# A two-block transformer kernel on one core: the memory attention's output weights are loaded before two modulation blocks, and their split is taken out of the attention

## The reference, cut to what matters

```
def mem_cross_attention(h, mem_n, w_q, w_kv, q_gain, k_gain, w_out):
    q = rmsnorm((h @ w_q).reshape(Bn, S, X_HEADS, X_HEAD_DIM), q_gain)
    k, v = jnp.split(mem_n @ w_kv, 2, axis=-1)
    k = rmsnorm(k.reshape(Bn, M, X_HEADS, X_HEAD_DIM), k_gain)
    s = einsum('bqhd,bkhd->bhqk', q, k) * (X_HEAD_DIM ** -0.5)
    p = softmax(s)
    o = einsum('bhqk,bkhd->bqhd', p, v).reshape(Bn, S, D_MODEL)
    return o @ w_out

for l in range(DEPTH):        # DEPTH = 2
    x = x + mixer_l(...)
    x = x + mem_cross_attention(rmsnorm(x, norm_mem_q[l]), rmsnorm(mem, norm_mem_kv[l]), ...)
    x = x + swiglu(rmsnorm(x, norm_ffn[l]), ffn_w_gu[l], ffn_w_down[l])
```

## Time and profile before

| what | value |
|---|---|
| runs | 2614.1 us median (2608.96, 2614.1, 2616.44) |
| the profiled execution | 2612.99 us, its span 2611.2 us |
| PE / DVE / ACT / POOL busy | 84% / 66% / 46% / 12% of the span |
| output projection begins, layer 0 | 279.87 us |
| ff-0 issued / its split on ACT begins, layer 0 | 291.29 / 300.71 us |
| TensorE resumes for the feed-forward's norm, layer 0 | 306.27 us |
| the same three in layer 1 | 798.62, 810.00 / 819.39, 824.95 us |

### The profile page before, as it was taken

One profiled execution on the slowest core, in us unless ns is written; L12 is line 12 of the kernel. 1 busy time (PEld: TensorE's weight loads), 2 busy tenths in 40 slices (PEclk: granted clock), 3 DMA queues, 4 the chain that ended last, 5 costly groups with the idle time before them and its releaser, 6 DMA issues. The chain is left out here.

```text
span 2611.2 us, 30694 instructions
## 1 busy us (share of the span) xinstructions
PE 2181.6 (84%) x11338; PEld 1616.0 (62%) x11338; DVE 1725.5 (66%) x2101; ACT 1212.2 (46%) x1436; POOL 305.9 (12%) x396
## 2 busy tenths in 40 slices
PE   6989899896998998987968888888568688888884
PEld 5777687785776876764745555555455555555552
DVE  5667554445675545467568777777576578887785
ACT  3333343333333442256246666666316266666663
POOL 2000000100000000000211211111120121211121
PEclk9989999997999999999979999999789799999997
DMA  8745464561655645410569999999710689999993
GB/s 274 256 149 194 153 208 168 186 238 65 236 188 172 199 159 205 142 31 1 218 262 402 406 414 405 406 411 381 237 23 11 254 363 408 416 416 407 411 415 149
DMA packets 175983, 655.21 MB, mean 251 GB/s; under 512 B 17680, under 2 KB 63200, under 8 KB 150544
## 3 DMA queue, kind: packets, MB, share of 16 engines
q1 hardware_dynamic: 157888, 618.45, 62.1%
q0 software_dynamic: 16752, 32.20, 3.8%
q10 hardware_dynamic: 1248, 3.25, 0.3%
HBM read 653.64 MB, written 21.17 MB: 258 GB/s over the span
## 5 line engine op out<-in xcount | busy, mean ns | idle before, releaser
L609 PE MATMUL bank<-sb_ring_rounded,sb_hT_rounded 128*128 128x512 f32 x2672 | 675.0, 397 | 13.1 <-DVE sb_hT_rounded L1681 7.3
L609 PEld LDWEIGHTS bank<-sb_ring_rounded,sb_hT_rounded 128*128 128x128 f32 x2672 | 506.1, 191 | 121.9 <-DVE sb_hT_rounded L1681 8.8
L1126 PE MATMUL bank<-sb_ring_rounded,sb_arena_rounded 128*128 128x512 f32 x1024 | 426.8, 417 | 0.0
L1694 DVE TENSOR_TENSOR sb_ring_rounded<-sb_ring,sb_ring_rounded 128x2048 fp32r<-128x2048 f32 (+1 forms) x144 | 319.5, 2258 | 161.2 <-ACT sb_ring_rounded L1232 160.9
L2388 DVE TENSOR_TENSOR sb_ring_rounded<-sb_ring,sb_hT_rounded 128x2048 fp32r<-128x2048 f32 x128 | 287.6, 2288 | 169.1 <-ACT sb_hT_rounded L1560 168.2
L1232 ACT ACTIVATE sb_ring_rounded<-sb_ring 128x2048 fp32r<-128x2048 f32 (+1 forms) x144 | 264.2, 1885 | 249.1 <-PE bank L609 140.2
L1126 PE MATMUL bank<-sb_hT_rounded,sb_arena_rounded 128*128 128x512 f32 x512 | 234.7, 458 | 149.2 <-DVE sb_arena_rounded L2392 149.2
L609 PE MATMUL bank<-sb_ring_rounded,sb_arena_rounded 128*128 128x512 f32 x1168 | 310.9, 392 | 2.0 <-issue 2.0
L1126 PEld LDWEIGHTS bank<-sb_hT_rounded,sb_arena_rounded 128*128 128x128 f32 x512 | 113.1, 221 | 227.2 <-issue 181.3
L609 PEld LDWEIGHTS bank<-sb_ring_rounded,sb_arena_rounded 128*128 128x128 f32 x1168 | 220.0, 189 | 48.5 <-issue 2.6
L1560 ACT ACTIVATE sb_hT_rounded<-sb_ring 128x2048 fp32r<-128x2048 f32 x128 | 236.8, 1898 | 17.2 <-DMA sb_ring<-in_w_gate 17.2
(11 more groups left out here) (327 smaller groups left out, 2762.4 us busy)
## 6 DMA issues: line engine op xcount, KB each, us to landing
sb_ring<-in_w_gate SPq DMA_DIRECT2D x64, 2048.0 KB, 14.0
sb_ring<-in_w_up SPq DMA_DIRECT2D x64, 2048.0 KB, 14.7
sb_ring<-in_w_down SPq DMA_DIRECT2D x64, 2048.0 KB
sb_ring<-in_w_ada SPq DMA_DIRECT2D x48, 1024.0 KB, 7.4
sb_ring<-in_ffn_w_gu SPq DMA_DIRECT2D x44, 1024.0 KB, 7.8
sb_ring<-in_xa_w_kv SPq DMA_DIRECT2D x16, 1024.0 KB, 7.3
sb_ring<-in_ffn_w_down SPq DMA_DIRECT2D x16, 1024.0 KB, 6.2
sb_ring<-in_od_w_in SPq DMA_DIRECT2D x12, 1024.0 KB, 8.0
```

The costliest lines, as they stand in the source:

```text
L609: ins = pe.matmul(bank[b][0:rows, :], rnd(x), rnd(w[:, k, :]), start=start and k == k0 and q == 0, stop=stop and k == k1 - 1 and q == len( ...
L1126: ins = pe.matmul(bank[2 * j + part][:, :], rnd(mxT[:, j, kk, :]), rnd(w), start=kk == 0 and q == 0, stop=kk == KD - 1 and q == 1)
L1694: dve.tensor_tensor(rnd(w), w, whole(high_of(n)[:, k0:k1, :]), ALU.subtract).then_inc(*c.up(s["w_lo"]))
```

## The change

It does three things, in both layers of the first block. (1) In `loads`, out-a comes ahead of ada-1 and ada-2 and no longer behind them. `uses` is unchanged. (2) ScalarE splits out-a whole, two halves, right after TensorE has begun v-1. (3) VectorE takes its first half between the two tiles of the queries' norm, and its second half behind the attention's transposed result. The quarters inside the attention are gone there; the other attention that uses them (`even_mixer`) keeps them.

```diff
         loads, uses, loads_to, uses_to = [], [], {}, {}
+        loaded_first = {first[name] for name in ("xa_out0", "xa_out1", "qkv0")}
         for n in range(len(stream)):
             rows = [("ada", k) for k in modulated_before.get(n, ())]
-            loads += [("w", n)] + rows if n == first["qkv0"] else rows + [("w", n)]
+            loads += [("w", n)] + rows if n in loaded_first else rows + [("w", n)]
             uses += rows + [("w", n)]
@@ ScalarE, cross(l)
-                    if i < 5:
-                        ahead(first[f"xa_k{l}"] + i)
+                    ahead(first[f"xa_k{l}"] + i)
@@
-                attention(xa_jobs, None, first[f"xa_out{l}"])
+                attention(xa_jobs)
@@ VectorE, cross(l)
                 dve.wait_ge(*c.next(s["proj_act"]))
-                for t in range(2):
-                    prepare(xa_q, t, 0)
+                prepare(xa_q, 0, 0)
+                split(first[f"xa_out{l}"], (0,))
+                prepare(xa_q, 1, 0)
                 copied(5)
@@
-                attention(xa_jobs, first[f"xa_out{l}"])
+                attention(xa_jobs)
                 turned([0, 1])
+                split(first[f"xa_out{l}"], (1,))
                 residual(first[f"xa_out{l}"], [(0, t) for t in range(2)])
```

## The result

The changed kernel takes 2628.1 us (median of 11 runs, 2620.1 to 2632.0), the kernel before in the same comparison 2612.8 (11 runs). The ratio is 1.0063, 95% interval 1.0053 to 1.0073: slower by 16.5 us (13.8 to 19.1). The forecast was 13.5 us, just under that interval, and 2627.6 us. The profiled executions have spans of 2626.9 and 2611.2 us, 15.7 apart.

What follows compares the result with a forecast made beforehand. No engine is full; TensorE's restart hangs on ff-0's landing, with no slack. Per layer -3.98 + 10.73 = +6.75 us, +13.5 over both layers, on 2614.1 gives 2627.6 us, range 2619 to 2634.

Steps and rivals of the forecast that it cites:

- Quarters out: Memory attention without VectorE's quarters: four steps at TensorE's pace of 1.95 us, ending 4.54 us earlier per layer.
- VectorE's first half in front: Split half ahead of the second tile's norm: the attention starts 0.56 us later, of 2.33 us added.
- The second half behind the result: VectorE's 2.33 us behind the attention's result, covered by the projection's first 12 matmuls (2.76 us): cost 0.
- ScalarE's whole split: About 3.7 us after v-1 has begun, inside ScalarE's idle of 5.41 us: cost 0.
- Out-b's begin: Second half of the output projection: begins 3.98 us earlier, the gain of 4.54 less the loss of 0.56.
- Two blocks ahead of ff-0: At out-b's begin ada-3 and ada-4 go out before ff-0, delaying its landing 10.73 us at 391 GB/s.
- The rest of the stage: Behind ff-0's landing: nothing further on has a time of its own, so everything moves along with the later restart.
- The tail: From ff-0's landing to TensorE's restart: a fixed 5.56 us, unchanged.
- ff-1's wait: TensorE's 5.27 us idle for ff-1, issued at TensorE's begin of ada-3 in both kernels: it moves along.
- that rival: Feed-forward gives part back: a later start shortens ff-1's wait, 1.5 us per layer, 2617 in all; chance 7%.
- the hidden transfer: Out-b's matmuls and the norm cover three blocks, the 3.98 us gain stays twice: 2606.1 us; chance 5%.
- The clock: TensorE's restart behind longer idle: already at the lower clock, so cost 0, bounds -1 and +1.5 us.

Runs made afterwards that it cites:

- E2: The kernel before with only the split's new places and no quarters in the attention, its order of loads kept; 2603.2 us, ratio 0.998.
- e1: The kernel before with only out-a loaded ahead of ada-1 and ada-2, quarters kept in the attention; 2632.0 us against 2609.9, ratio 1.0089.
- e9: The changed kernel run once more, unaltered, against the kernel before; 2625.9 us, ratio 1.0065.
- e3: The changed kernel with ff-0 also ahead of ada-3 and ada-4 in the list of loads; 2617.1 us, ratio 1.0028.
- e5: The changed kernel with ff-0 between ada-3 and ada-4 in the list of loads; 2621.5 us, ratio 1.0056.
- e4: The kernel before with only ff-0 moved ahead of ada-3 and ada-4 in the list of loads; 2611.1 us, ratio 1.0005.
- e6: The kernel before with only ff-0 moved between ada-3 and ada-4 in the list of loads; 2600.4 us, ratio 0.9973.

## Why the prediction was right

**Quarters out: as forecast.** 4.54 us a layer was forecast, the four steps give 12.34 - 7.79 = 4.55. TensorE does set the pace without them: in the windows below it is busy 13.77 of the 14 us from 256 to 270, where it was busy 10.55. E2, with the old order of loads, has the same A.

**VectorE's first half in front: as forecast.** From v-1's begin to the first exponential 21.28 us before, 21.86 after: +0.58 against +0.56. The second half behind the result costs nothing: TensorE's idle in front of the projection is 1.46 us in both kernels. ScalarE's whole split (233.09 to 236.81) ends 1.52 us before the copy behind it: cost 0.

**Out-b's begin: as forecast.** Against v-1's begin it is 59.85 us before and 55.88 after, -3.97 against -3.98; that it agrees so closely is luck (see the clock below).

**Two blocks ahead of ff-0: right in place, a little too small.** Forecast 10.73 us, measured 20.77 - 9.42 = 11.35 in layer 0 and 20.44 - 9.39 = 11.05 in layer 1. This is the mis-sized term. Windows of TensorE's busy time, then PEclk, DMA share, GB/s: the changed kernel while the pair flows and then while ff-0 flows, and the kernel before while ff-0 flows.

```profile
291.00:301.00 10.00, 8.47 (x38) 1.00 1.04 392
301.50:307.00 5.50, 0.00 (x0) 0.69 1.10 350
```

```profile
293.00:298.50 5.50, 5.50 (x26) 1.00 1.07 358
```

The rate that I took for the pair was right: at 392 GB/s its 4.194 MB take 10.70 us, and at layer 1's 388 (817 to 827 us) 10.81. What the term lacks is that ff-0's own 9.42 us don't stay as they were. Behind the pair ff-0's data come at 350 GB/s and not 358, in layer 1 at 349 (828 to 833) and not 365 (812 to 817, before). By estimate, 2.097 MB at these rates, that is 0.13 and 0.26 us. It covers layer 1's excess over 10.81 us; in layer 0 another 0.5 us is left, which I can't place. The Trainium skill (DMA: Bandwidth & Descriptors, Bandwidth) has 341 GB/s for 1 MB, with which the pair would cost 12.3 us, an estimate; the measured pair lies between that and my 10.73, and the trace disagrees with that rate: it shows 392.

**The rest of the stage: as forecast.** The tail is 5.55 us (5.56), the transposes take 1.97 as before, the modulation block 5.40 (5.36), ff-1's wait 5.29 (5.27). From layer 0's restart to v-1 of layer 1 it is 443.51 us before and 443.84 after, and from layer 1's restart to the end 1786.25 and 1785.79. So the feed-forward gives nothing back, and that rival is out, as is the hidden transfer (15.70 us of idle, where it needed 4.4 or less).

**The clock: put at 0, and 0 in the sum by luck.** Two parts that I had not seen cancel. A fell by 5.58 us, not 3.98, and the projection grew by 1.60. TensorE's windows (us, busy, PEclk, DMA share, GB/s), first before:

```profile
256.00:270.00 14.00, 10.55 (x51) 1.00 0.01 2
270.00:276.00 6.00, 4.82 (x18) 0.72 0.00 0
276.00:280.00 4.00, 1.49 (x10) 1.00 0.00 2
280.00:290.00 10.00, 10.00 (x45) 1.00 0.59 210
```

and the changed kernel:

```profile
256.00:270.00 14.00, 13.77 (x69) 1.00 0.01 1
270.00:276.00 6.00, 2.87 (x19) 1.00 0.00 0
276.00:280.00 4.00, 4.00 (x11) 0.57 0.00 0
280.00:290.00 10.00, 10.00 (x45) 1.00 0.02 1
```

The granted clock fell to its lower level (1.2 GHz) once in each of these stretches. Before, it fell in the attention's last values (8 matmuls in 3.43 us; 1.99 in the changed kernel). Afterwards it fell at the projection's begin (23.64 us for 96 matmuls, not 22.04). The fall stands in the next stage, at the same price, and out-b's begin comes out at the forecast's 3.98. That it moved isn't shown to be the change's doing: e1, with the quarters in place, has a fall in layer 1's projection too (23.39 us), and the changed kernel run again (e9) has none in layer 1 (22.05).

**What of the 15.7 us is left.** The stretches give +7.37 and +6.93 us a layer; the forecast was +6.75. The other 1.4 us of the span come from ahead of layer 0's stretch, in code that is the same, where half a modulation block in the mixer (64 matmuls) took 3.38 us at 116.24, and 1.95 in the trace of before, at 116.66. The causes are shown by e1 (the order alone: +23 us), e2 (the split alone: -5) and the row of e3, e5 and the changed kernel (5.5 us a block). Where my understanding did fail was in e3 and e4: I followed ff-0's slot and not what comes after it in that slot, one more turn of the same ring.

## What to carry to other kernels

Moving one load ahead in a ring changes whom every later item follows. Write down, for each slot, the item that follows it before and after the move, and when the one ahead is released. In a queue that issues in order, the latest of these holds back all behind it. Look for the block whose wait ends on the critical path, and bring that one forward by as little as it needs: here one place won 7 us (e6), two places won nothing (e4), and two places for a block that nobody waited for lost 23 us (e1).

## What the runs showed of the hardware that was not expected

The same code took different times by where the granted clock fell. The stretch A has the same instructions in before, e1, e4 and e6, and takes 34.78 or 34.79 us four times in eight, 35.99 once and 37.74 or 37.75 three times; without the quarters it takes 30.81 to 30.83 five times and 32.06 to 32.70 otherwise. e1's windows over layer 0's stretch (columns as in the earlier trace rows):

```profile
246.00:256.00 10.00, 7.59 (x64) 6.09 (x53) 4.80 (x14) 3.77 (x11) 0.00 (x0) 1.00 0.46 176
256.00:268.00 12.00, 9.26 (x46) 7.16 (x45) 8.88 (x22) 6.25 (x14) 0.00 (x0) 1.00 0.00 0
268.00:280.00 12.00, 7.60 (x40) 5.56 (x39) 7.28 (x14) 6.29 (x9) 0.00 (x0) 1.00 0.01 2
```

The clock is 1.00 throughout, where before's trace has 0.72 in 250 to 256 and again in 270 to 276. Two falls in A cost 2.96 us there, and a single one 1.2 to 1.9 us in the other traces. At full clock the two forms of the attention are 34.79 - 30.81 = 3.98 us apart, the very sum of the forecast. Which executions fall and which don't, no run here explains.

TensorE's idle before the restart also has a price of its own. After 0.75 us of idle the eight transposes take 1.09 us and the modulation block 3.70 (e4, e6). After 4.20 us or more the transposes take 1.97 in every trace, and the block between 4.28 (e2) and 5.72 us (e3), at a granted clock of 0.59 in the kernel before. A longer idle makes it no worse: behind 15.7 us the block takes 5.40, behind 4.67 and 4.70 us (e3) 5.68 and 5.72. The changed kernel's window behind its 15.70 us (columns as above) reads

```profile
315.00:317.00 2.00, 1.83 (x8) 1.57 (x8) 1.95 (x4) 0.60 (x1) 0.00 (x0) 0.50 0.00 0
```

One such restart costs 0.88 us in the transposes and 0.6 to 2.0 in the block, 2.5 and 2.6 us together in the kernel before. The Trainium skill (TensorE: Matmul & The Clock Gate, HAM oscillation) says that a matmul stage that keeps waiting for transfers restarts at the low clock each time. The traces agree: all 16 restarts of these stages behind 4.20 us of idle or more have their transposes at 1.97 us.
